# Twenty products on a constant in the opening, and another order for four modulation pieces

## What is computed

```python
mod = jax.nn.silu(c) @ ada_w + ada_b                 # 9 x 6144, in fp32
sh_m, sc_m, g_m, sh_f, sc_f, g_f = split(mod, 6)
xn = _rmsnorm(x, norm_mix_g) * (1.0 + sc_m) + sh_m
xa, ga, pu, pv = split(xn @ w_in, 4)                 # 512 columns each
h = rg_lru(conv(xa)); ya = h * gelu(ga)              # gates r and i, a scan over time
yb = gelu(pu) * spatial_gate(rmsnorm(gelu(pv)))
x = x + g_m * (group_rmsnorm([ya, yb]) @ w_out)
xn = _rmsnorm(x, norm_ffn_g) * (1.0 + sc_f) + sh_f
x = x + g_f * moe(xn)                                # top 8 of 64 experts, one shared
```

## Time and profile before

| | |
|---|---|
| time, median of 3 runs | 798.7 us (798.02 to 800.08) |
| the profiled execution: its own time / its span | 799.33 us / 797.6 us |
| PE busy | 700.1 us (88%) |
| DVE / ACT / POOL busy | 41% / 28% / 38% |
| mean granted TensorE clock | 0.976 |
| HBM read and written over the span | 375 GB/s |

### The profile page before, as it was taken

How to read it: one execution, slowest core, us unless ns; L and a number is a source line. 1 busy time by engine, 2 the same in 40 slices (tenths; PEclk the granted TensorE clock), 3 DMA queues, 4 the chain that set the end, 5 groups by cost and what they waited for, 6 DMA issues and landing times.

```text
span 797.6 us, 15126 instructions
## 1 busy us (share of the span) xinstructions
PE 700.1 (88%) x5157; PEld 408.9 (51%) x5158; DVE 328.7 (41%) x615; ACT 225.2 (28%) x389; POOL 301.3 (38%) x317
## 2 busy tenths in 40 slices
PE   4999899999999999999999989998789977997930
PEld 3765556446555446545565656454355543543510
DVE  3262278477344552344323332434323433243217
ACT  5130612023223331233223222323222332232212
POOL 0050112021306544545544562636435454455130
PEclk9999999999999999999999999999999999999975
DMA  8976998829689999999999999999999999999943
GB/s 335 416 219 231 350 345 300 346 79 386 223 329 381 393 411 370 340 382 391 395 381 395 387 396 404 387 407 399 408 414 401 400 400 410 398 402 402 359 99 130
DMA packets 60206, 279.15 MB, mean 350 GB/s; under 512 B 18997, under 2 KB 20289, under 8 KB 32764
## 3 DMA queue, kind: packets, MB, share of 16 engines
q1 hardware_dynamic: 36520, 252.35, 78.3%
q0 software_dynamic: 23424, 26.07, 13.7%
q10 hardware_dynamic: 212, 0.08, 0.0%
HBM read 272.54 MB, written 26.30 MB: 375 GB/s over the span
## 4 chain that ended last, share of the span: by engine, by line
PE 61%; DMA 28%; DVE 5%; issue 3%; SPq 1%; ACT 1%; POOL 0%; POOLq 0%; DVEq 0%; ACTq 0%
PE bank L1140 25%; DMA gu<-in_exp_w_up 24%; PE bank L1176 10%; PE bank L854 4%; PE bank L872 4%; PE bank L1003 4%; PE bank L1118 2%; DMA gu<-in_ada_rest 2%; PE bank L842 2%; PE bank L913 1%; PE bank L875 1%; PE bank L1232 1%; DMA gu<-in_mix_w 1%; PE bank L1157 1%; PE bank L1087 1%
## 5 line engine op out<-in xcount | busy, mean ns | idle before, releaser
L1140 PE MATMUL bank<-gu,et 128*64 128x256 f32 x2496 | 283.3, 380 | 32.0 <-DMA gu<-in_exp_w_up 26.8
L1140 PEld LDWEIGHTS bank<-gu,et 128*64 128x64 f32 x2496 | 188.9, 137 | 144.0 <-issue 73.4
L544 POOL DMA_INDIRECT acc_rows<-et,idx x64 | 104.6, 1634 | 242.4 <-DVE et L1667 141.4
L1176 PE MATMUL bank<-dn,et 128*64 128x512 f32 x632 | 150.6, 601 | 12.4 <-issue 10.0
L1660 DVE COPY et<-bank 128x256 f32<-128x256 f32 x64 | 27.2, 424 | 255.7 <-PE bank L1157 234.8
L737 ACT ACTIVATE et<-bank 64x512 f32<-64x512 f32 x64 | 37.8, 591 | 261.9 <-PE bank L1140 237.3
L1176 PEld LDWEIGHTS bank<-dn,et 128*64 128x64 f32 x632 | 42.7, 136 | 78.0 <-issue 76.9
L747 ACT ACTIVATE et<-bank,mb 128x512 f32<-128x512 f32 x64 | 44.0, 687 | 120.3 <-PE bank L1176 98.2
L1667 DVE TENSOR_SCALAR et<-bank,mb 128x512 f32<-128x512 f32 x64 | 48.1, 751 | 68.3 <-PE bank L1176 54.4
L1653 DVE TENSOR_TENSOR et<-et 64x512 f32<-64x512 f32 x64 | 67.9, 1061 | 0.5 <-ACT et L738 0.4
L554 POOL DMA_DIRECT2D small<-halfc x49 | 56.3, 1148 | 0.0
(11 more groups left out here) (289 smaller groups left out, 622.1 us busy)
## 6 DMA issues: line engine op xcount, KB each, us to landing
dn<-in_exp_w_down SPq DMA_DIRECT2D x64, 1024.0 KB
gu<-in_exp_w_gate SPq DMA_DIRECT2D x63, 1024.0 KB
gu<-in_exp_w_up SPq DMA_DIRECT2D x63, 1024.0 KB
gu<-in_ada_rest SPq DMA_DIRECT2D x8, 2048.0 KB, 11.0
gu<-in_mix_w SPq DMA_DIRECT2D x4, 2048.0 KB, 12.9
gu<-in_lru_in_w SPq DMA_DIRECT2D x4, 1024.0 KB, 15.0
gu<-in_sgu_in_w SPq DMA_DIRECT2D x2, 2048.0 KB, 13.8
gu<-in_out_w SPq DMA_DIRECT2D x2, 2048.0 KB, 11.5
```

What stands on the lines that cost most here:

```text
L544: pool.indirect_dma_start(acc_rows[u % 2], bass.IndirectOffsetOnAxis(ap=idx[:, u, 0:1], axis=0), yo[:, u % 2, 0, :], None, bounds_check=2 ...
L1140: mm = pe.matmul(bank[u % 2][64 * c:64 * c + 64, b * FE:(b + 1) * FE], xt[:, b, k % 4, k // 4, :], w[c][:, k * FE:(k + 1) * FE], start=(k ...
L1176: mm = pe.matmul(bank[5 + b][64 * c:64 * c + 64, :], hT[:, b, j, :], dn[:, dslot(u), j * D + c * HALF:j * D + (c + 1) * HALF], start=(j == ...
```

## The change

PE gets 20 products of `ident` with `ones` (128 x 128 by 128 columns, fp32) into `bank[1]`, after the turn of c and before its wait for the small constants. Nobody reads them. In the middle, v's second tile goes ahead of `ada(4)`, `ada(5)` follows `ada(4)` directly instead of standing between the gates r and i, and u's first tile goes ahead of `ada(7)` instead of behind it. SP issues piece 7 (once `ada(5)` has been used) ahead of piece 8 (once v's third tile is done), where it was behind it.

```diff
@@ sync @@
             sync.wait_ge(s["mod_ready"], 1)
             load("ada", 6, io["ada_rest"][2])
+            sync.wait_ge(s["mod_ready"], 2)
+            load("ada", 7, io["ada_rest"][3])
             sync.wait_ge(s["prj_ready"], prj_no[("v", 2)] + 1)
             load("ada", 8, io["ada_rest"][4])
-            sync.wait_ge(s["mod_ready"], 2)
-            load("ada", 7, io["ada_rest"][3])
             sync.wait_ge(s["mod_ready"], 3)
@@ tensor @@
             mm.then_inc(s["tp_ready"], 1)
+            for k in range(20):
+                pe.matmul(bank[1][:, 0:P], ident[:, :], ones[:, :], start=True, stop=True)
             pe.wait_ge(s["ld_gb"], 32)
@@ tensor @@
             tokens("v", 3, 0)
+            tokens("v", 3, 1)
             ada(4)
-            tokens("v", 3, 1)
+            ada(5)
             tokens("v", 3, 2)
             pe.wait_ge(s["ld_rg"], 64)
             pe.wait_ge(s["conv_done"], 1)
             gates("r", wr)
-            ada(5)
             gates("i", wi)
@@ tensor @@
             ada(6)
+            tokens("u", 2, 0)
             ada(7)
-            tokens("u", 2, 0)
             ada(8)
             ada(9)
```

## The result

The changed kernel takes 804.47 us (median of 17 runs) where the kernel before takes 799.86 (median of 17, taken beside it). The ratio is 1.0057, 95% interval 1.0043 to 1.0072: 4.6 us slower, between 3.4 and 5.8. The profiled execution has a span of 802.3 us (before 797.6) and a mean granted clock of 0.966 (before 0.976).

The account below looks back on a forecast made before the run. The prediction took TensorE's chain, with waits for pieces 4 and 7, to bound the kernel up to the expert-weight stream, which passes on every delay. Terms 0.4 + 1.5 + 1.65 = 3.55 took 798.7 to 802.3 us; range 799.0 to 805.0.

Parts of the forecast that it names:

- 0.4 + 1.5 + 1.65 = 3.55: Forecast loss in us: opening 0.4, group means waiting longer for DVE 1.5, lower clock behind that idle time 1.65.
- three signs of being wrong: L977 (group means) ahead of 114 us, mod(7) waiting less than before, or the opening products keeping the clock up to mix(1).
- I take it as slow as before: Opening: mix(1) was assumed to stay at 3.57 us and a granted clock of 0.50, behind the token turns.
- the clock stays up through the token turns: Rival, opening: mix(1) runs fast, 1.5 us less than each other case, 800.8 for the forecast; chance 0.20.
- +0.4 forecast: Opening: net cost of the 20 products in us, with mix(1) starting 0.5 late and staying slow.
- forecast +0.98: v's third tile ends 0.98 us later: 1.95 for ada(5) less 1.03 for the wait for piece 4.
- The rival that the clock falls in it: Clock falls in the 2.2 us gap ahead of gates i, costing up to 1.65 us more: 804.0; chance 0.20.
- the 106 that I had worked out: Landing time in us of piece 9, with pieces of 2 MB arriving one after the other at some 5.2 us each.
- the step that carries the forecast: u's first tile ahead of ada(7) delays mod(7) and the scan on DVE, idling TensorE 4.8 us: +1.5 and +1.65.
- forecast 1.5 + 1.65 = 3.15: Middle: u's tile 1 later by 1.5 us through the wait for DVE, plus 1.65 for the lower clock behind it.
- the bounds given (0 to 2.4): Lower-clock cost behind the idle time ahead of the group means: 0 us if the clock holds, 2.4 if long low.
- Carried to the end one for one: Expert weight stream: every shift at 120 us was carried to the end in full, nothing given back.

Follow-up runs that it names:

- opening_nine: The kernel before with 9 products on the constant in the opening instead of the change's 20, nothing else changed: 801.6 us against 799.7.
- opening_again: The kernel before with only the 20 products in the opening, run a second time: 802.3 us against 798.6 before.
- opening_wait_filled: The kernel before with the 20 opening products and 15 more between ada(6) and ada(7), in the wait for piece 7: 799.9 us against 798.6.
- filler_before_means: The changed kernel with 13 more products behind ada(9), in TensorE's idle time ahead of the group means: 801.7 us against 798.9 before.
- opening_only: The kernel before with only the 20 products in the opening, first run: 801.7 us against 799.9 before.
- seven_first: The changed kernel with ada(7) ahead of u's first tile again: 797.6 us against 799.9 before.
- mod7_behind_no_products: The changed kernel with mod(7) moved behind the scan on DVE and without the 20 opening products: 797.4 us against 798.9 before.
- before_wait_filled: The kernel before with 10 products between ada(6) and ada(7), in the wait for piece 7, none in the opening: 799.1 us against 799.7.

## Why the prediction was right, point by point

**The time.** Forecast 802.3 from 798.7, that is +3.6; measured +4.6 (3.4 to 5.8), and 804.5 lies in the range of 799.0 to 805.0. Sign, range and the mechanism in the middle hold. That the number came out near is luck in part. The terms were 0.4 + 1.5 + 1.65 = 3.55. In the profiles they are -0.70, 0.78 and 2.07, together 2.15, and another 3.15 came later for which there was no term. Of the three signs of being wrong that I had named, one appeared in its effect: the clock was up at `mix(1)`, though the kernels without the products show that it wasn't the products that kept it there.

**The opening.** The 20 products ended at 13.49, forecast 14.0, and `mix(0)` ended at 16.08 instead of 16.9, but the token turns waited for xn as forecast (17.14 against 17.9). (The windows show a granted clock of 1.00 in the opening even over the slow `mix(0)` of before; what is said of its clock goes by its 3.64 us against 1.95.) The step that failed is "I take it as slow as before" for `mix(1)`. In all eight profiles with the 20 products it took 1.95 or 1.96 us. More telling are the four others without any: it took 1.95 or 1.96 in each of them too. The slow `mix(1)` of the profile before, on which both the hope for a gain and my term rested, was one case in five, and the rival "the clock stays up through the token turns", with a chance of 0.20, is what the profiles with the products show. The rule of the Trainium skill ("TensorE: Matmul & The Clock Gate", Part 4: PE-mode transpose), by which the clock would be lost again over the token turns, was not borne out by these eight, nor by the four, in which `mix(0)` was slow (3.39 to 3.64) and the clock came up by `mix(1)` all the same. In opening_nine alone `mix(0)` took 1.95 and `mix(1)`, behind the same turns, 3.35. So the term was +0.4 forecast and -0.7 in the trace at v's first tile, and by the four about nothing. Alone, the lead was lost again at piece 7, and twice the kernel came out slower by 2 to 3 us. Part of that seems to be the clock behind the longer wait (1.75 us in the traces of opening_again and opening_wait_filled, 1.9 in times that overlap). The mean clocks of all executions fit that, 0.9695 against 0.972, and 0.972 again with the wait filled. But why it ends behind the kernel before, which has a slow `ada(7)` in its profile as well, stays open.

**v, ada(4), ada(5).** The wait for piece 4 went. From v's start to the gates r it is 21.06 us where it was 20.61: +0.45, forecast +0.98. The term was mis-sized in two places: v's two tiles take 13.83 us to the next product when they follow one another, not 2 x 7.06, and `ada(4)` with `ada(5)` takes 3.63, not 3.9.

**The gap ahead of the gates i.** 2.21 us, released by ACT: as forecast. The rival that the clock falls in it had 0.20; in one profile of six it did so, just behind the gap.

**Pieces 7 and 9.** No wait for piece 7. Pieces 7 and 8 landed at 94.6 and 100.4, near the 95 and 100 forecast. Piece 9, issued at 97.15, took 11.7 us and TensorE waited 1.14 us for it, to 108.9 instead of the 106 that I had worked out. It landed 8.4 us after piece 8, not 5.2; why is not shown. It cost nothing, since the idle time behind it only shrank.

**u ahead of ada(7).** This is the step that carries the forecast, and its mechanism stood: `mod(7)` late, 8.59 forecast and 8.58 measured to the square, the means starved. From v's start, u's tile 2 begins 2.85 us later than before (61.45 against 58.60), forecast 1.5 + 1.65 = 3.15. Of it 2.07 is the clock, by filler_before_means, within the bounds given (0 to 2.4) and above the value taken. That leaves 0.78 for the longer wait, half of the 1.5 forecast. Some 0.5 of the difference comes from v, `ada(4)` and `ada(5)` above. Here too the two errors cancel.

**What the sum had no term for.** At 126.69 us the changed kernel is 2.15 us late, at the first expert product 5.3. The other 3.15 come between 188.4 and 210.8 us, where products of the shared expert and of the router run slowly. The granted clock is 0.50 from about 188.6 to 192 and again from about 202 to 209; before has one such stretch there, from about 199 to 203. PE's timeline of the changed kernel, then the same two rows of before:

```profile
188.44 2.00 PE L872 MATMUL bank<-gu,xT 128*128 128x512 f32 x2
190.37 1.86 PE L1049 MATMUL bank<-late,xT 128*64 128x64 f32 x16
```

```profile
186.29 1.12 PE L872 MATMUL bank<-gu,xT 128*128 128x512 f32 x2
187.34 1.15 PE L1047 MATMUL bank<-late,xT 128*64 128x64 f32 x16
```

Windows of the changed kernel, the columns as above:

```profile
186.00:188.00 2.00, 1.84 (x18) 1.70 (x18) 1.93 (x3) 0.00 (x0) 0.00 (x0) 1.00 0.98 412
188.00:190.00 2.00, 2.00 (x10) 0.80 (x8) 0.29 (x3) 1.69 (x3) 1.95 (x5) 0.64 1.05 442
```

The table shows that the three kernels with the lowest clock in the middle (0.91) have 0.85 here, and those with 1.00 there have 0.90 to 1.00 here. opening_only fits less well, with 0.95 in the middle and 0.85 here. It also fits the timed runs, in which moving `mod(7)` gained some 3 us more than the middle gives, and the mean clocks of all executions. With one profile of each kernel that is a pattern and no cause: whether the one fall brings the other, or both come from how the work lies in time, is open.

**Carried to the end one for one.** Shown by the same table: 5.3 us at the expert stage, 4.7 in the span.

## What to carry to other kernels

Before moving work on one engine past a piece that another engine consumes in a fixed order, look at what that other engine has queued behind the piece: here u's tile filled TensorE's wait and starved the scan, and undoing that, by one line moved on the consumer (`mod(7)`) or by `ada(7)` put ahead of u's tile again, turned +4.6 us into -3.4 and -3.0. A slow product behind an idle gap is only a target if it is slow in several profiles; here the one profile of before showed a slow `mix(1)` that four others didn't have. And look for the next wait for a transfer behind a gain: a lead of 1.09 us ahead of the wait for piece 7 was 0.21 us late behind it.

## What the runs showed of the hardware that I had not expected

The granted clock fell to 0.50 around idle gaps of TensorE of very different length, and not always inside them. In seven_first it fell behind 1.89 us ahead of the means, 1 us after they had begun. In one of six profiles it fell behind the 2.21 us ahead of the gates i, in mod7_behind_no_products some 0.4 us into them. It fell in all six profiles that have 2.99 us or more ahead of piece 7 or of the means with nothing to fill them. So a gap of 2 us is a risk and not a price. Nor is a gap always needed: at 188.6 us in the changed kernel the clock fell though TensorE had not been idle for more than 0.43 us at a time since 180 us.

Each fall around a gap in the middle cost 1.3 to 2.6 us. The most is in opening_nine, where `ada(7)` and u's first tile took 11.51 us to the next product; in before_wait_filled they took 8.95.

Piece 7 took 10.6 to 11.0 us from issue to landing in the four kernels with products in the opening and the old order behind it, and 9.4 in the two of that order without them; why the opening should reach that far is not known.
